# A memory accumulator for expert rows: weights applied before an adding scatter, GpSimd copying its own slots, and diagonal rows fetched with the pairs

## The reference, cut to what matters

```python
h = rmsnorm(x, norm1_g) * (1.0 + sc1) + sh1
x = x + gt1 * hybrid_mixer(h, ...)            # x1 below
h = rmsnorm(x, norm2_g) * (1.0 + sc2) + sh2   # h2 below
x = x + gt2 * hierarchical_moe(h, ...)
return rmsnorm(x, normf_g)

# hierarchical_moe, for each token:
g_sel = argmax(group logits); p_group = softmax(group logits)[g_sel]
top_v, top_i = lax.top_k(e_logits of that group, 2)
wts = p_group * softmax(top_v)
# for each of the two experts e:
hid = silu(xb @ w1[e]) * (xb @ w3[e])
y  += wts * (hid @ w2[e])
```

## Time and profile before

| what | value |
|---|---|
| median of three runs | 2004.72 us (2001.64 to 2007.18) |
| profiled execution | 2005.42 us |
| its span | 2003.4 us |
| PE busy | 1940.9 us (97%) |
| PEld busy (weight loads of PE) | 1616.6 us (81%) |
| DVE busy | 1346.3 us (67%) |
| ACT busy | 941.5 us (47%) |
| POOL busy | 207.4 us (10%) |
| memory read, written | 348.50 MB, 49.67 MB |

### The profile page before, as it was taken

How to read it: one execution, slowest core, us unless ns; L and a number is a source line. 1 busy time by engine, 2 the same in 40 slices (tenths; PEclk the granted TensorE clock), 3 DMA queues, 4 the chain that set the end, 5 groups by cost and what they waited for, 6 DMA issues and landing times.

```text
span 2003.4 us, 28051 instructions
## 1 busy us (share of the span) xinstructions
PE 1940.9 (97%) x9687; PEld 1616.6 (81%) x9687; DVE 1346.3 (67%) x1786; ACT 941.5 (47%) x1279; POOL 207.4 (10%) x179
## 2 busy tenths in 40 slices
PE   6999999999999999999999999997999999999996
PEld 5788888888888888888888788886888888888882
DVE  6545454111758568577585545667999999999996
ACT  5211111111444525535345243214878887878863
POOL 0000000000110010010100000001222222222210
PEclk7999999999999999999999999997999999999998
DMA  8242423221323222232232659427999999999966
GB/s 315 68 125 74 147 73 106 76 64 62 101 76 81 72 70 80 67 98 67 63 83 72 208 192 307 145 101 294 374 378 381 382 378 387 380 389 384 397 257 255
DMA packets 220504, 382.11 MB, mean 191 GB/s; under 512 B 49909, under 2 KB 162982, under 8 KB 194982
## 3 DMA queue, kind: packets, MB, share of 16 engines
q1 hardware_dynamic: 202566, 333.89, 47.9%
q10 hardware_dynamic: 8672, 30.76, 4.0%
q0 software_dynamic: 9216, 16.80, 2.2%
HBM read 348.50 MB, written 49.67 MB: 199 GB/s over the span
## 4 chain that ended last, share of the span: by engine, by line
PE 61%; issue 25%; DMA 4%; DVE 4%; POOL 3%; ACT 2%; SPq 1%; ACTq 0%; POOLq 0%; DVEq 0%
PE ps L710 25%; PE ps L2775 17%; PE ps L2819 9%; PE ps L2670 4%; PE ps L2761 1%; POOL X L784 1%; POOL decay L777 1%; PE ps L2799 1%; DMA so_lo<-o_lo_d 1%; POOL decay L780 1%; PE ps L2692 1%; DMA ada_sh<-in_w_ada_dram 1%; DMA y_t<-y_d 0%; DMA out_dram<-res 0%; DMA xg<-h_d,tok_now 0%
## 5 line engine op out<-in xcount | busy, mean ns | idle before, releaser
L605 DVE TENSOR_TENSOR mw_lo<-mw_raw,mw_hi 128x2048 fp32r<-128x2048 f32 x192 | 436.8, 2289 | 43.2 <-ACT mw_hi L600 42.9
L710 PE MATMUL ps<-h_hi,w_lo 128*128 128x512 f32 x1152 | 462.0, 401 | 0.5 <-DVE h_lo L1572 0.5
L710 PE MATMUL ps<-h_hi,w_hi 128*128 128x512 f32 x1152 | 449.2, 390 | 0.0
L710 PE MATMUL ps<-h_lo,w_hi 128*128 128x512 f32 x1152 | 448.7, 389 | 0.0
L600 ACT ACTIVATE mw_hi<-mw_raw 128x2048 fp32r<-128x2048 f32 x192 | 368.1, 1919 | 115.3 <-PE ps L2775 66.0
L710 PEld LDWEIGHTS ps<-h_hi,w_hi 128*128 128x128 f32 x1152 | 216.2, 188 | 45.7
L710 PEld LDWEIGHTS ps<-h_hi,w_lo 128*128 128x128 f32 x1152 | 216.8, 188 | 41.0 <-DVE h_lo L1572 0.6
L710 PEld LDWEIGHTS ps<-h_lo,w_hi 128*128 128x128 f32 x1152 | 216.8, 188 | 39.3
L671 DVE TENSOR_TENSOR w_lo<-w_raw,w_hi 128x1024 fp32r<-128x1024 f32 x88 | 107.6, 1223 | 155.4 <-ACT w_hi L666 154.3
L2775 PE MATMUL ps<-mw_hi,xT_lo 128*128 128x512 f32 x512 | 203.5, 397 | 3.2 <-DVE xT_lo L2207 2.4
L2775 PE MATMUL ps<-mw_hi,xT_hi 128*128 128x512 f32 x512 | 200.7, 392 | 0.0
(11 more groups left out here) (402 smaller groups left out, 3044.8 us busy)
## 6 DMA issues: line engine op xcount, KB each, us to landing
mw_raw<-in_w_dram SPq DMA_DIRECT2D x192, 1024.0 KB, 7.7
w_raw<-in_w_in_dram SPq DMA_DIRECT2D x72, 512.0 KB, 4.2
ada_b<-in_w_ada_dram SPq DMA_DIRECT2D x8, 2048.0 KB, 7.9
y_t<-y_d SPq DMA_DIRECT2D x7, 1024.0 KB, 10.5
ada_sc<-in_w_ada_dram SPq DMA_DIRECT2D x4, 1024.0 KB, 8.7
w_raw<-in_w_proj_b_dram SPq DMA_DIRECT2D x8, 512.0 KB, 4.2
merged_b_d<-sc_y ACTq DMA_DIRECT2D x8, 512.0 KB, 2.6
decay<-crow_d SPq DMA_DIRECT2D x8, 512.0 KB, 5.9
```

What stands on the lines that cost most here:

```text
L605: dve.tensor_tensor(mw_lo[off % NSPLIT][:], mw_raw[off % NRAW][:], mw_hi[off % NSPLIT][:], ALU.subtract).then_inc(mw_lo_done, 1)
L710: last = pe.matmul(dst, lhs[:, s, k], rhs[:, k, cols], start=(k == 0 and part == 0), stop=(k == KD - 1 and part == 2))
```

## The change

- y_d and the two loads of it, turn_w, the pair products of PE and both DVE steps on them are gone. A new memory array acc_d (1024 rows) takes x1: SP stores it, eight tiles of 512 KB, in the output projection (store_x1), the last two tiles after the first four weight chunks.
- Each expert's rows are weighted before they are scattered. ACT's copy_y takes the weight of each slot, wt_now, as its scale; POOL multiplies y_sb by gt2_row. The scatter then adds rows in memory (compute_op add) at acc_d, by token. Since two blocks may hold the same token, each scatter waits until the one before it has landed. The last block is weighted by DVE in one operation from PSUM.
- wt_now is fetched for each block by a new indirect DMA (fetch_weights, one 4-byte row per slot) from wts_d, a memory array that ACT writes after block_act(0); weights() is therefore moved to just before block_dve(0). POOL waits for this store, and for x1's, ahead of its first fetch.
- POOL makes the copies out of ids itself: tok_now in gather, slot_now (both destinations) in fetch_weights. DVE's two are gone.
- In the tail SP loads acc_d, 4 MB, and ACT's square, root, DVE's reciprocal and scaling follow directly.
- In the heads, inv_rows is issued right behind pair_first, without the wait for base_step, and DVE's first pair operation waits for all of them (160 in place of 144).

```diff
@@ POOL
...
-            def scatter(b, s):
+            def gather(b, s, before, first=False):
+                if not first:
+                    pool.wait_ge(xg_in[s], 16 * before)
+                    pool.tensor_copy(tok_now[:, s:s + 1], ids[:, 1, bass.ds(b, 1)]).then_inc(tok_ready, 1)
...
+            def fetch_weights(b, s, before):
+                wait_from(pool, y_out[s], 16 * before)
+                pool.tensor_copy(slot_now[:, :, s], ids[:, :, bass.ds(b, 1)].rearrange("p z o -> p (z o)"))\
+                    .then_inc(pair_ready, 1)
                 pool.wait_ge(pair_ready, b + 1)
                 pool.sem_inc(waits_passed, 1)
-                pool.indirect_dma_start(y_d, bass.IndirectOffsetOnAxis(pair_now[:, s:s + 1], axis=0), y_sb[:, s], None,
-                                        bounds_check=TOP_K * T - 1, oob_is_err=False).then_inc(y_out[s], 16)
+                pool.indirect_dma_start(wt_now[:, s:s + 1], None, wts_d, bass.IndirectOffsetOnAxis(slot_now[:, 0, s:s + 1], axis=0),
+                                        bounds_check=TOP_K * T - 1, oob_is_err=False).then_inc(wt_in[s], 16)
+            def scatter(b, s, before, weighted=None):
+                pool.wait_ge(y_copied, b + 1)
+                if weighted is not None:
+                    pool.tensor_tensor(y_sb[:, s], y_sb[:, s], gt2_row[:], ALU.mult).then_inc(y_weighted, 1)
+                    pool.wait_ge(y_weighted, weighted)
+                wait_from(pool, y_out[1 - s], 16 * before)
+                pool.sem_inc(waits_passed, 1)
+                pool.indirect_dma_start(acc_d, bass.IndirectOffsetOnAxis(slot_now[:, 1, s:s + 1], axis=0), y_sb[:, s], None,
+                                        bounds_check=T - 1, oob_is_err=False, compute_op=ALU.add).then_inc(y_out[s], 16)
...
+            pool.wait_ge(acc_in, 16 * (TT + 1))
+            pool.wait_ge(rows_in, 16 * 7)
+            def two_blocks(i):
+                fetch_weights(2 * i, 0, i)
+                gather(2 * i + 3, 1, i + 1)
+                scatter(2 * i, 0, i, 2 * i + 1)
+                fetch_weights(2 * i + 1, 1, i)
+                gather(2 * i + 4, 0, i + 2)
+                scatter(2 * i + 1, 1, i + 1, 2 * i + 2)
...
@@ SP
-                sp.wait_ge(base_step, OPS * h + SUB_OPS + 1)
                 sp.dma_start(inv_rows[:], inv_d[0].rearrange("t p j -> p t j")).then_inc(base_moved, 16)
...
+            def store_x1(n):
+                sp.dma_start(acc_d[n * P:(n + 1) * P, :], x1[:, n]).then_inc(acc_in, 16)
...
+                sp.dma_start(y_t[:, n], acc_d[n * P:(n + 1) * P, :]).then_inc(tile_in[n % 4], 16)
@@ ACT
-                act.activation(y_sb[:, s], ps[:, bank:bank + 2].rearrange("p a d -> p (a d)"), ACT.Copy)\
-                   .then_inc(y_copied, 1)
+                act.wait_ge(wt_in[s], 16 * (before + 1))
+                act.activation(y_sb[:, s], ps[:, bank:bank + 2].rearrange("p a d -> p (a d)"), ACT.Copy,
+                               scale=wt_now[:, s:s + 1]).then_inc(y_copied, 1)
...
             block_act(0)
+            act.wait_ge(r_step, R_WTS)
+            act.dma_start(wts_d.rearrange("(n p k) o -> p n (k o)", p=P, k=TOP_K), wts[:]).then_inc(acc_in, 16)
@@ DVE
-                dve.wait_ge(base_moved, moved(h, 144))
+                dve.wait_ge(base_moved, moved(h, 160))
...
+            weights()
+            block_dve(0)
...
-            weights()
+            dve.wait_ge(rows_in, 16 * 7)
+            dve.wait_ge(y_copied, NE - 1)
+            dve.wait_ge(y_out[1], 16 * (NE // 2 - 1))
+            dve.wait_ge(wt_in[1], 16 * (NE // 2))
+            dve.wait_ge(mw_used, PER * NE)
+            dve.scalar_tensor_tensor(out=y_sb[:, 1], in0=ps[:, 2:4].rearrange("p a d -> p (a d)"), scalar=wt_now[:, 1:2],
+                                     in1=gt2_row[:], op0=ALU.mult, op1=ALU.mult).then_inc(y_copied, 1)
             over_table(src)
```

More of the change, by code:

```diff
@@ L396, in decoder_block @@
     top[0] = R1
[L397 removed]
+    y_t = at("y_t", [P, TT, D])
     assert top[0] <= R2
     top[0] = R2
[L400 to L401 removed]
     y_sq = at("y_sq", [P, D])
[L403 removed]
     stat3 = at("stat3", [P, 3, TT])
@@ new lines, in _ @@
+            two_blocks(0)
+            with pool.Fori(1, NE // 2 - 2) as i:
+                two_blocks(i)
+            fetch_weights(NE - 4, 0, NE // 2 - 2)
+            gather(NE - 1, 1, NE // 2 - 1)
+            scatter(NE - 4, 0, NE // 2 - 2, NE - 3)
+            fetch_weights(NE - 3, 1, NE // 2 - 2)
+            scatter(NE - 3, 1, NE // 2 - 1, NE - 2)
+            fetch_weights(NE - 2, 0, NE // 2 - 1)
+            fetch_weights(NE - 1, 1, NE // 2 - 1)
+            scatter(NE - 2, 0, NE // 2 - 1, NE - 1)
@@ L1071, in _ @@
                 load_chunk(sp, 0, 0, off, off)
+            for n in range(TT - 2, TT):
+                sp.wait_ge(x1_done, past(2 + 2 * n + 2))
+                store_x1(n)
             def load_block(b, e_next):
@@ new lines, in _ @@
+            for n in range(TT):
+                dve.wait_ge(x1_root, TT + n + 1)
+                dve.reciprocal(stat3[:, 2, n:n + 1], stat3[:, 1, n:n + 1]).then_inc(x1_inv, 1)
+                dve.wait_ge(x1_inv, TT + n + 1)
+                for cols in (slice(0, D),) if n < TT - 1 else (slice(0, HALF), slice(HALF, D)):
+                    dve.scalar_tensor_tensor(out=y_t[:, n, cols], in0=y_t[:, n, cols], scalar=stat3[:, 2, n:n + 1],
+                                             in1=nf_row[:, cols], op0=ALU.mult, op1=ALU.mult).then_inc(res_done, 1)
@@ L2853, in _ @@
             over_blocks(pe, over_pe, blocks_over)
-            idle_products(4, 5)
-            pe.wait_ge(ids_ready, 3)
-            for n in range(TT):
-                pe.wait_ge(w_turned, TOP_K * (n + 1))
-                if n:
-                    pe.wait_ge(tile_in[n % 4], tile_arrivals(n))
-                if n >= 4:
-                    pe.wait_ge(acc_step, 2 * (n - 4) + 3)
-                for half in range(2):
-                    if n == 0:
-                        pe.wait_ge((first_half_in, tile_in[0])[half], (16, tile_arrivals(0))[half])
-                    cols = slice(half * HALF, (half + 1) * HALF)
-                    for k in range(TOP_K):
-                        last = pe.matmul(ps[:, 2 * (n % 4) + half], turn_w[:, k, n], y_t[:, n, k, cols],
-                                         start=(k == 0), stop=(k == TOP_K - 1))
-                    if n == 0 and half == 0:
-                        last.then_inc(y_summed, 1)
-                last.then_inc(y_summed, 1)
 _INS = ['x', 'c', 'w_ada', 'b_ada', 'norm1_g', 'w_in', 'conv_qkv_w', 'a_log', 'dt_bias', 'onorm_g', 'w_proj_a',
```

126 lines of the change are left out of this document (33 added, 93 removed).

## The result

The changed kernel takes 2025.95 us (median of 4 runs, 2024.32 to 2028.98), the kernel before 2005.7 beside it: a ratio of 1.0104, 95% interval 1.0092 to 1.0117, some 20 us slower. The profiled execution has a span of 2022.6, against 2003.4. The ratio comes from all the runs, so it isn't exactly the quotient of the medians. The forecast was 2014: the side was right, the size (9 us) less than half of it.

A forecast was written before the change was run, and what follows sets the result against it. PE, busy 97% of the span, was taken as the bound, with DVE's 1.30 us of air per block as the margin. 2005.4 - 8 + 0 + 18 + 18 - 19 = 2014.4, less 0.7: 2014 us, range 1992 to 2042.

The forecast's parts named there:

- A: Head stage: diagonal rows fetched with the pairs remove most of PE's waits for X; -8 us (0 to -10.5).
- B: Output projection: storing x1 to memory, with weights() moved before block 0, costs nothing; 0 us (0 to +3).
- C: Start of the experts: the weights' store in 8-byte pieces lands late and delays copy_y(0); +18 us (+3 to +20).
- D: Expert blocks: POOL's product holds up DVE, making 18.3 us per block; +18 us (0 to +38).
- rival 3: Expert blocks: the serial chain through POOL sets the pace; 2026 to 2049 us, 2040 as one value; chance 0.15.
- E: Tail: pair products, DVE steps and half of the loads go, block 31's weighting is added; -19 us (-15 to -22).
- Rival 1: Expert blocks: POOL's hold, at most 1.6 us, fits into DVE's air and costs nothing; 1996 us; chance 0.20.
- Rival 2: Start of the experts: the small store passes the weights in a bunch, costing some 5; 2001 us; chance 0.13.
- Rival 4: Heads: nothing gained, as POOL's earlier X products collide with DVE's; 2022 us; chance 0.07.

The follow-up runs named there:

- e3: The changed kernel with a scatter that overwrites instead of adding, POOL's product kept: 2013.82 us, ratio 1.0035.
- e1: The kernel before with only the edit in the heads (inv_rows issued behind pair_first, the pair step waits for it too): 2001.71 against 2006.75 us, ratio 0.9974.
- e7: The changed kernel with acc_d filled in the head stage by eight copies of x, no stores of x1 during the output projection: 2023.96 us, ratio 1.0079.
- e6: The changed kernel with the store to wts_d made of 16 pieces of 512 bytes, from another tile: 2018.7 us, ratio 1.0061.
- e4: The changed kernel with an overwriting scatter and without POOL's product of y_sb and gt2_row: 1993.89 us, ratio 0.9935.
- e9: The changed kernel with an overwriting scatter and POOL's product over half of the columns: 1996.33 us, ratio 0.9949.
- e10: The changed kernel with block 31's scatter overwriting a memory array of its own, without waiting for block 30's: 2023.73 us, ratio 1.0088.
- e8: The kernel before with the edit in the heads and gt2 applied by DVE straight from PSUM in place of ACT's copy: 1997.3 against 2006.84 us, ratio 0.9952.
- e2: The changed kernel without POOL's product of y_sb and gt2_row, the adding scatter kept: 2028.11 us, ratio 1.0102.

## The prediction against the result

**What bounds the kernel.** PE, as said. But the earlier trace rows has two figures near their limit, DVE's 16.42 and the DMA share of 1.00, and the argument took only the first as a bound. This is the step that failed: the scatter that adds was priced by its landing alone and put at nothing as a load on the DMA engines. The runs show a second limit of about 18.9 us per block in its place. e3, without the addition, takes 2013.82, close to the 2014 forecast, which is in part luck (see the range).

**A, forecast -8, measured -5.7 in the profile and -5.2 by e1.** The chain was right: inv_rows at 622.70, the X products done at 631.6 (forecast 631.3). The -5.7 of one trace is at the early end of its spread; e1, with its eleven runs, excludes the 8. The mis-sized term is what PE gets of it: "would go in most of them" holds for the waits named, but 2.7 for Y, 3.6 before L2557 and 2.5 for X stand in their place.

**B, forecast 0 (0 to +3), measured +2.7.** Inside its bounds; the value taken was the wrong end. The share of 0.60 was read in one window. That the stores of x1 lengthen the routing is shown by e7 and by the range over all kernels; that they do it by delaying the store of h and the gathers, on which PE waits, is argued.

**C, forecast +18 (+3 to +20), measured +10.0.** The mechanism holds by e6, and the price was too high: the store took 15.2 us, less the 2.6 of a store that is alone over 64 pieces 0.2 us per piece, not 0.3 to 0.7. It landed at 1416.6, and the weight loads didn't need to run dry first. So PE stood for 9.0 us and not 16; the low clock behind it cost 1.5 of the 2 forecast. In the other runs the store's landing was 9.8 to 20.9 us, 0.1 to 0.3 per piece. The Trainium skill ("DMA: Bandwidth & Descriptors", section "Queues, rings and completion order") has an engine take turns between queues by whole packets. The forecast's reading of it, one or two turns and the start at 5 or less, takes the section's ceiling of 64 descriptors in a packet, and isn't borne out. The same section calls 9 to 17 typical. As an estimate from that figure, 64 pieces are 4 to 8 turns and one piece per engine is one, and 15.2 and 4.5 us speak neither against that nor prove it: no run shows the size of a packet. What sets the 0.2, and its spread, stays open.

**D, forecast +18 (0 to +38), measured +26.6.** The first half of the blocks is the forecast, 18.30 for 18.3. Its parts are a little other: a hold of 1.8 and not 2.1, and 0.4 of DVE's waits for ACT that don't vanish with it. e3, e4 and e9 show this mechanism. The rest, about 0.6 more per block in the last ten, is the addition in memory: e3 has none of it, and 548.3 from copy to copy in place of 556.0. By the estimate above it takes the DMA engines 0.8 us more per block, and the pace becomes 18.9. The buffers of weights seem to hide this at first, while the time to landing grows from 9.5 to 13.9 us; ACT's waits for weights then pass it on. The text priced the adding scatter as a latency (the landing, in rival 3 and in part E) and never as occupancy.

**E, forecast -19 (-15 to -22), measured -15.1.** From the first load to the end the forecast had 1984.2 - 1959.4 = 24.8, and it is 2022.6 - 1997.9 = 24.7. That is luck: the first tile took 3.6 in place of 4.1 and the seven others 1.7 each in place of 1.9, and the end came 6.5 behind the last root in place of 4.4. What failed is "scatter 31 starts at 1953.9", which leaves out the chain: it has to wait for the landing of scatter 30, 5.73 us here. From the copy of block 30 to the first load the forecast had 1959.4 - 1943.9 = 15.5, measured 19.7; e10 takes this wait away and has 15.3, but only half of it reaches the end, so e10 shows about 2 of the 3.9 us to come from the chain.

**The rivals.** Rival 1 was right in form: a hold of 0.7 costs the blocks nothing (e9), and neither does 1.22 of DVE's own work (e8), but the hold is 1.8. Where between them the edge lies no run shows; with 0.4 of waits that don't vanish it would be nearer to 1.2 than to the 1.6 of the rival. With the adding scatter it would not have helped, as e2 shows. Rival 2 is between: C cost 10, neither 18 nor 5. Rival 3 gave 2026 to 2049, and the time is inside; its mechanism isn't there, for POOL waited for y_sb in every block, 108.4 us in 31 by the page; a scatter waited for the landing of the one before once, 5.7 us, and ACT for a fetch twice, 10.2 us. The right number came from another cause. Rival 4 falls with e1.

**The range,** 1992 to 2042, held 2026, on the side that was forecast; the forecast's own, 2003 to 2026, just so. The sum is a small difference of large terms, 8 + 19 against 18 + 18, so the misses weigh: of the 10.2 us that lie between +9 and +19.2, A has 2.3, B 2.7, D 8.6, E 3.9 and a stretch without a forecast 0.7, and C took 8.0 back. D's miss is the second limit. Without it the sum would have come out near the forecast only because C's miss happens to cancel those of A, B and E.

## What to carry to other kernels

Read every resource of the window that bounds a stage, and not only the engine that the change loads: with DVE at 93% and the DMA engines at 100%, a change that adds to both meets two limits, and taking one away shows nothing while the other stands. Price an operation that reads and writes in memory by the time it takes of the DMA engines as well as by its landing, and count the rows that it really moves: the last blocks here had three halves of the average. Work that can be given to DVE straight from PSUM may be cheaper than the same work on POOL in SBUF: 1.22 us here against a hold of 1.8.

## What the runs showed of the hardware

- Two scatters that add, of some 195 rows of 4 KB in all, take the DMA engines 5.2 us; two that overwrite the same rows take 2.0. Over all 32 blocks, with 64 rows on average, the addition costs them 0.8 us per scatter.
- POOL's two-input product of 128x1024, 2.35 us alone, holds DVE for 1.6 (mean over all blocks, by the splits) to 1.8 us, at half width for 0.6 to 0.7. The other way round POOL waits as well: its product shows 3.5 to 3.7 us and a copy of two columns 1.3 in place of 0.18.
- POOL's issue of a scatter, 0.97 alone, shows 1.58 in a block of the kernel before, where DVE is busy 93%, and 4.44 in e8, where DVE is busy 98%, though DVE's splits are none the longer for it (2288 ns for 2289). Whether it is DVE that draws it out, and how, isn't settled by these runs.
- 1024 pieces of 8 bytes amid weight loads landed in 9.8 to 20.9 us, 16 pieces of 512 bytes in 4.5.
